# The last output product of every stage split by columns around the first turning of the next input

## The reference

```python
x = x + rms_norm(concat(gated, attention, conv) @ w_out, post_mix_g)        # moba
x = x + rms_norm(cross_attention(rms_norm(x, pre_x_g), m), post_x_g)        # cross
x = x + rms_norm(square(relu(rms_norm(x, pre_ffn_g) @ w_ff1)) @ w_ff2, g)   # relu
for i in range(2):                                                          # second block
    h = h + 0.5 * rms_norm(swiglu(rms_norm(h, g[0])), g[1])                 # glu0, glu2
    u = rms_norm(h, g[2])
    m = diff_attention(u) if i == 0 else neighborhood_attention(u)          # diff, near
    h = h + rms_norm(m, g[3])
    h = h + 0.5 * rms_norm(swiglu(rms_norm(h, g[4])), g[5])                 # glu1, glu3
```

## Time and profile before

| | |
|---|---|
| median of three runs | 1430.43 us |
| time of the profiled execution | 1429.05 us |
| its span in the trace | 1427.3 us |
| TensorE (PE) matmul busy | 1386.7 us (97%) |
| VectorE (DVE) busy | 816.4 us (57%) |
| ScalarE (ACT) busy | 704.5 us (49%) |
| GpSimd (POOL) busy | 144.3 us (10%) |
| granted TensorE clock | 0.997 of full |
| DMA, mean | 179 GB/s |

### The profile page before, as it was taken

The page is one execution under the profiler, slowest core; times in us unless marked ns, Lnnn a source line. Parts: engine busy times, 40 slices in busy tenths (PEclk is TensorE's granted clock), DMA queues, the critical chain, the costliest instruction groups (busy, mean ns, idle before and its releaser), DMA issues.

```text
span 1427.3 us, 17574 instructions
## 1 busy us (share of the span) xinstructions
PE 1386.7 (97%) x7129; PEld 1162.9 (81%) x7129; DVE 816.4 (57%) x900; ACT 704.5 (49%) x911; POOL 144.3 (10%) x254
## 2 busy tenths in 40 slices
PE   6999999999999999999999999999999999999996
PEld 6998788888888888877778888888888777788885
DVE  4986745645565444565765445654555556654552
ACT  5637654544455434465754444444344666544341
POOL 1000101111101111000111110021160100000000
PEclk9999999999999999999999999999999999999998
DMA  9854434865557655553348556485655533465530
GB/s 310 269 171 148 133 133 137 254 191 195 190 163 227 196 198 184 176 192 123 128 135 252 186 193 200 163 228 190 206 180 177 192 118 134 146 223 178 198 125 30
DMA packets 123421, 255.87 MB, mean 179 GB/s; under 512 B 6280, under 2 KB 36812, under 8 KB 123340
## 3 DMA queue, kind: packets, MB, share of 16 engines
q1 hardware_dynamic: 119244, 251.58, 54.3%
q0 software_dynamic: 4096, 3.15, 0.8%
HBM read 253.66 MB, written 1.05 MB: 178 GB/s over the span
## 4 chain that ended last, share of the span: by engine, by line
PE 88%; DVE 4%; ACT 3%; issue 3%; DMA 1%; POOL 0%; SPq 0%; DVEq 0%; POOLq 0%; ACTq 0%
PE ps L1159 25%; PE ps L1161 25%; PE ps L1160 25%; PE ps L1426 2%; ACT w_hi L595 2%; DVE w_lo L836 2%; PE ps L1147 1%; PE ps L1149 1%; PE ps L1148 1%; PE ps L1225 1%; DVE x_rows L883 1%; PE ps L1188 1%; PE ps L1265 1%; DMA raw<-w_in 1%; ACT t L654 1%
## 5 line engine op out<-in xcount | busy, mean ns | idle before, releaser
L836 DVE TENSOR_TENSOR w_lo<-raw,w_hi 128x2048 fp32r<-128x2048 f32 x226 | 518.5, 2296 | 423.4 <-ACT w_hi L595 422.9
L595 ACT CAST w_hi<-raw 128x2048 fp32r<-128x2048 f32 x226 | 430.3, 1907 | 396.7 <-PE ps L1161 382.4
L1159 PE MATMUL ps<-w_hi,hT_hi 128*128 128x512 f32 (+1 forms) x1168 | 442.1, 378 | 6.7 <-DVE w_lo L836 6.7
L1161 PE MATMUL ps<-w_hi,hT_lo 128*128 128x512 f32 (+1 forms) x1168 | 436.6, 374 | 0.0
L1160 PE MATMUL ps<-w_lo,hT_hi 128*128 128x512 f32 (+1 forms) x1168 | 436.0, 373 | 0.0
L1159 PE MATMUL ps<-w_hi,yT_hi 128*128 128x512 f32 (+1 forms) x672 | 258.3, 384 | 0.0
L1159 PEld LDWEIGHTS ps<-w_hi,hT_hi 128*128 128x128 f32 x1168 | 220.0, 188 | 46.6 <-DVE w_lo L836 8.6
L1161 PE MATMUL ps<-w_hi,yT_lo 128*128 128x512 f32 (+1 forms) x672 | 255.1, 380 | 0.0
L1160 PE MATMUL ps<-w_lo,yT_hi 128*128 128x512 f32 (+1 forms) x672 | 254.8, 379 | 0.0
L1161 PEld LDWEIGHTS ps<-w_hi,hT_lo 128*128 128x128 f32 x1168 | 219.9, 188 | 39.6
L1160 PEld LDWEIGHTS ps<-w_lo,hT_hi 128*128 128x128 f32 x1168 | 220.2, 189 | 37.1
(11 more groups left out here) (157 smaller groups left out, 1029.5 us busy)
## 6 DMA issues: line engine op xcount, KB each, us to landing
raw<-ffn_wg SPq DMA_DIRECT2D x44, 1024.0 KB, 5.5
raw<-ffn_wu SPq DMA_DIRECT2D x44, 1024.0 KB, 5.4
raw<-ffn_wd SPq DMA_DIRECT2D x44, 1024.0 KB, 5.2
raw<-w_ff SPq DMA_DIRECT2D x32, 1024.0 KB, 5.8
...
```

Of the source, the lines that this page charges most:

```text
L595: act.copy(hi_part(c), raw[:, c % NRAW, :]).then_inc(hi_done, 1)
L836: dve.tensor_tensor(lo_part(c), raw[:, c % NRAW, :], hi_part(c), ALU.subtract).then_inc(lo_done, 1)
L1159: pe.matmul(o, hi, wh[:, i, cols], start=first and i == 0, stop=False)
L1161: ins = pe.matmul(o, lo, wh[:, i, cols], start=False, stop=last and i == len(tiles) - 1)
```

## The change

Three things are changed in the words, and the code learns the new ones.

1. The last product word of every stage but glu3 is split by columns, and `turn0` with it: `d5.1a sq0 turna0 d5.1b post2 turnb0`. `turna0` is the turning of b = 0, `turnb0` that of b = 1. `sq0` now stands ahead of the turning. In moba the last product was `o2.1`, with `turn0 sq0` ahead of it. In diff, near and cross `turn0` stood ahead of `o3.1`, in relu ahead of `s da7.1 db7.1`.
2. `post2` is `post` for t = 1, now at the stage's end, ahead of `turnb0`. At the next head a new word `add1` does both additions to x for t = 1, ahead of the first split, and `gain1` does its two multiplications alone.
3. `HEAD_QK` (diff and near) has the split behind `tq0.1` moved behind `rk0.1`, where two now stand. In diff's fill table the casts `h` of step 2 and of steps 5 to 8, and the subtractions `l` of steps 6 to 9, stand later (the last cast in step 10, the last subtraction in step 11).

```diff
-HEAD_GLU = ("ga0.0 post1 s gb0.0 gain1 s ua0.0 turn1 sq1 ub0.0 G0.0 H0.0 ga0.1 s gb0.1 G0.1 s ua0.1 s "
+HEAD_GLU = ("ga0.0 add1 s gb0.0 gain1 s ua0.0 turn1 sq1 ub0.0 G0.0 H0.0 ga0.1 s gb0.1 G0.1 s ua0.1 s "
...
-           "tq0.1 s kb0.1 rk0.1 s va0.0 tk0.1 va0.1 h ")
+           "tq0.1 kb0.1 rk0.1 s s va0.0 tk0.1 va0.1 h ")
...
-    "glu1": GLU + "post0 gain0 da4.1 s db4.1 turn0 sq0 d5.1",
+    "glu1": GLU + "post0 gain0 da4.1 s db4.1 d5.1a sq0 turna0 d5.1b post2 turnb0",
...
-                                   5: "||h l|vd0.1 rv1", 6: "||h l|o0.0", 7: "||h l|o0.1", 8: "||h l|o1.0", 9: "||l|o1.1a",
-                                   10: "|||o1.1b", 11: "|||o2.0a"}) +
+                                   5: "||l|vd0.1 rv1", 6: "||h|o0.0", 7: "||l|o0.1", 8: "h||l|o1.0", 9: "h|||o1.1a",
+                                   10: "h|l||o1.1b", 11: "|l||o2.0a"}) +
...
+TURN_HALVES = {"turn": (0, 1), "turna": (0,), "turnb": (1,)}
...
-            j = word.at - word.digit
-            return word.digit, j, j + 2 if j < N_NORMS - 1 else None
+            j = word.at - (word.digit == 1)
+            return min(word.digit, 1), j, j + 2 if j < N_NORMS - 1 else None
...
-            def turned_hi(n, t, dst):
-                for b in range(2):
+            def turned_hi(n, t, dst, halves=(0, 1)):
+                for b in halves:
...
-                    if n is None:
-                        for b in range(2):
-                            add_y(j, t, b)
+                if word.name == "add" or n is None:
+                    for b in range(2):
+                        add_y(j, t, b)
                 if word.name == "gain":
                     for b in range(2):
-                        add_y(j, t, b)
+                        if t == 0:
+                            add_y(j, t, b)
                         gain_row(n, x, t, b)
...
-            def turn(n, t):
+            def turn(n, t, halves=(0, 1)):
...
-                for b in range(2):
+                for b in halves:
                     pe.wait_ge(normed, 2 * (TT * n + t) + b + 1)
```

More of the change, by code:

```diff
@@ L73 @@
 GLU = HEAD_GLU + "".join(BLOCK_GLU.format(a=b - 1, b=b) for b in range(1, 5)) + LAST_GLU
-HEAD_RELU = ("ua0.0 post1 s ub0.0 gain1 s ua1.0 turn1 sq1 ub1.0 G0.0 H0.0 ua0.1 s ub0.1 G0.1 H0.1 s ua1.1 T0 s "
+HEAD_RELU = ("ua0.0 add1 s ub0.0 gain1 s ua1.0 turn1 sq1 ub1.0 G0.0 H0.0 ua0.1 s ub0.1 G0.1 H0.1 s ua1.1 T0 s "
              "ub1.1 G1.0 H1.0 G1.1 H1.1 s da0 s db0 s ")
@@ L78 @@
         "ua7 s T6 ub7 G7.0 H7.0 G7.1 H7.1 s da6.0 T7 db6.0 da7.0 db7.0 ")
-HEAD_QK = ("qa0.0 post1 s qb0.0 gain1 s sq1 rq0.0 ka0.0 turn1 kb0.0 tq0.0 rk0.0 qa0.1 s qb0.1 tk0.0 rq0.1 s ka0.1 "
-           "tq0.1 s kb0.1 rk0.1 s va0.0 tk0.1 va0.1 h ")
+HEAD_QK = ("qa0.0 add1 s qb0.0 gain1 s sq1 rq0.0 ka0.0 turn1 kb0.0 tq0.0 rk0.0 qa0.1 s qb0.1 tk0.0 rq0.1 s ka0.1 "
+           "tq0.1 kb0.1 rk0.1 s s va0.0 tk0.1 va0.1 h ")
 PLAN = {
@@ L86 @@
                                  5: "||h l l|o3.0"}) +
-             "o2.0 post0 gain0 o3.1 turn0 sq0 o2.1"),
-    "cross": ("qa0.0 post1 s qb0.0 gain1 s sq1 rq0.0 qc0.0 turn1 qd0.0 tq0.0 rq1.0 qa0.1 s qb0.1 tq1.0 rq0.1 s qc0.1 "
+             "o2.0 post0 gain0 o3.1 o2.1a sq0 turna0 o2.1b post2 turnb0"),
+    "cross": ("qa0.0 add1 s qb0.0 gain1 s sq1 rq0.0 qc0.0 turn1 qd0.0 tq0.0 rq1.0 qa0.1 s qb0.1 tq1.0 rq0.1 s qc0.1 "
               "tq0.1 h qd0.1 rq1.1 exp " +
               attention("cross", 4, {0: "tq1.1|||", 4: "||l h|o0.0", 5: "||l|o0.1", 6: "||h l|o1.0"}) +
-              "o2.0 o3.0 post0 gain0 o1.1 h l o2.1 turn0 sq0 o3.1"),
-    "relu": RELU + "post0 gain0 da6.1 s db6.1 turn0 sq0 s da7.1 db7.1",
-    "glu0": GLU + "post0 gain0 da4.1 s db4.1 turn0 sq0 d5.1",
+              "o2.0 o3.0 post0 gain0 o1.1 h l o2.1 o3.1a sq0 turna0 o3.1b post2 turnb0"),
+    "relu": RELU + "post0 gain0 da6.1 s db6.1 s da7.1 db7.1a sq0 turna0 db7.1b post2 turnb0",
+    "glu0": GLU + "post0 gain0 da4.1 s db4.1 d5.1a sq0 turna0 d5.1b post2 turnb0",
     "diff": (HEAD_QK +
-             attention("diff", 8, {0: "||l|vb0 rv0", 1: "||h l|qc0 qd0.0 rq1.0", 2: "||h|qd0.1 rq1.1 l kc0.0 tq1 kc0.1",
+             attention("diff", 8, {0: "||l|vb0 rv0", 1: "||h l|qc0 qd0.0 rq1.0", 2: "|||qd0.1 rq1.1 h l kc0.0 tq1 kc0.1",
                                    3: "|||kd0.0 rk1.0 kd0.1 h tk1.0 rk1.1 l vc0.0 tk1.1 vc0.1", 4: "||h|vd0.0",
-                                   5: "||h l|vd0.1 rv1", 6: "||h l|o0.0", 7: "||h l|o0.1", 8: "||h l|o1.0", 9: "||l|o1.1a",
-                                   10: "|||o1.1b", 11: "|||o2.0a"}) +
-             "h l o2.0b o3.0 post0 gain0 o2.1 turn0 sq0 o3.1"),
-    "glu1": GLU + "post0 gain0 da4.1 s db4.1 turn0 sq0 d5.1",
-    "glu2": GLU + "post0 gain0 da4.1 s db4.1 turn0 sq0 d5.1",
+                                   5: "||l|vd0.1 rv1", 6: "||h|o0.0", 7: "||l|o0.1", 8: "h||l|o1.0", 9: "h|||o1.1a",
+                                   10: "h|l||o1.1b", 11: "|l||o2.0a"}) +
+             "h l o2.0b o3.0 post0 gain0 o2.1 o3.1a sq0 turna0 o3.1b post2 turnb0"),
+    "glu1": GLU + "post0 gain0 da4.1 s db4.1 d5.1a sq0 turna0 d5.1b post2 turnb0",
+    "glu2": GLU + "post0 gain0 da4.1 s db4.1 d5.1a sq0 turna0 d5.1b post2 turnb0",
     "near": (HEAD_QK +
@@ L106 @@
                                  9: "||l|o2.0b"}) +
-             "o3.0 post0 gain0 o2.1 turn0 sq0 o3.1"),
+             "o3.0 post0 gain0 o2.1 o3.1a sq0 turna0 o3.1b post2 turnb0"),
     "glu3": GLU + "post0 da4.1 db4.1 d5.1 end1",
@@ L808, in _ @@
                         split()
-                    elif word.name in ("post", "sq", "turn", "end"):
+                    elif word.name in ("post", "sq", "end") or word.name in TURN_HALVES:
                         norm_word(word)
@@ L1120, in _ @@
                         split()
-                    elif word.name in ("post", "gain", "sq", "turn", "end"):
+                    elif word.name in ("post", "add", "gain", "end") or word.name in TURN_HALVES:
                         norm_word(word)
```

14 lines of the change are left out of this document (7 added, 7 removed).

## The result

| | before | after |
|---|---|---|
| median | 1430.43 us | 1415.11 us (1414.64 to 1416.05, four runs) |
| time of the profiled execution | 1429.05 us | 1414.64 us |
| its span | 1427.3 us | 1412.8 us |
| ratio to the kernel before | | 0.9894, 95% interval 0.9877 to 0.9912 |

A forecast was written before the change was run, and what follows sets the result against it. TensorE, busy for 1386.7 of 1427.3 us, was taken as the bound, so only shorter waits help. Terms -5.4 - 8.8 - 1.3 + 1.2 + 0.4 + 0.2 = -13.7 gave a median of 1416.7 us; 8-in-10 range 1414 to 1420.5.

The forecast's parts named there:

- Half turnings: Stage ends of moba, diff and near: all of the 1.79 us lost in waits for `t` goes at each, -5.4 us.
- Second switch of instruction: Turning split in two: TensorE's additional switch between transposes and product costs 0.1 to 0.3 us over eight heads, taken as +0.2.
- The low part for the next product: Next stage's first product: its `hT_lo` is ready with 0.16 us left, so the cost is counted as 0.
- `post2`: Stage's end: second square of y at 916.74, the cast then as before, GpSimd's root there at 918.47 and short.
- `add1`: Stage heads: with both additions ahead of the first split, eight waits for `w_lo` go, 1.10 us each, -8.8.
- The 0.4 for the third chunk: Stage heads: the third chunk's load must also come in ahead of a matmul, 0.05 us at each head, +0.4.
- Rival A: Heads: VectorE's chain runs without overlaps, a wait of 0.3 to 0.6 us a head stays, 1421.5; 0.23 together with Rival C.
- HEAD_QK and step 2: Rotations in HEAD_QK and diff's step 2 no longer stand behind a `w_lo` or cast; two waits for `gain` go, -1.3 us.
- diff's later steps: Diff's fill: moved casts hold squares `A5` to `A7`, `o3.0` starts at 719.2 instead of 717.9, early gain spent, +1.2 us.
- Rival B: Diff keeps what its first steps gain, as `A7` is not held: -2 instead of +1.2, 1413.5 us; chance 0.10.
- Rival C: Inside the stages half of the heads' gain is given back, 4.4 us, 1421; chance 0.23 together with Rival A.
- E: Whole kernel: the change alters nothing, since another wait already stands behind those that go, 1430 us; chance 0.04.

The follow-up runs named there:

- late split: The changed kernel with the split `s` moved behind `sq0` in the tails of glu0, glu1 and glu2: 1417.37 us, ratio to the kernel before 0.9917.

## Why the prediction held

**Half turnings (-5.4).** By starts 1.8 in each of moba, diff and near, and no `t` was late anywhere. The kernel with the split alone shows the term by itself: 5.05.

**Second switch of instruction (+0.2).** It came, though in two parts of opposite sign. The end of glu2, from its last turn to products with `hT` (1075.00 before, 1064.43 after) to near's first product, takes 30.14 us before and 30.04 after: four transposes cost 0.36 twice where eight cost 0.79. But the first half product of each head now stands right behind four transposes, and takes 2.84 (907.41 to the line below) where it took 2.72: the second matmul starts 0.31 behind the first, the next ones 0.23 to 0.24 apart.

```profile
910.25 0.39 PE L1162 MATMUL ps<-w_hi,hT_hi 128*128 128x512 f32 x1
```

Together it is 0.03 a stage, 0.2 over eight heads. The term was taken from no row, so its size is luck.

**The low part for the next product (0).** Slack predicted 0.16, measured 0.24. The late split shows what stands behind it.

**`post2`.** The second square was put 0.27 ahead of the next first product and came 0.16 ahead (907.25, 907.41). The prediction's own 0.36 for four transposes gives 0.16 (917.21 less 0.36, against 917.01); its 916.74 was a slip of 0.1. GpSimd's root behind it took 0.30 us (908.04) beside a scaling that reads PSUM (907.97 to 908.66), as predicted. Without this step being right, the sum would have been 11 us off, as the kernel with `post` at the head shows.

**`add1` (-8.8 + 0.4).** Additions, `w_lo` and multiplications ran with the predicted overlaps: 909.18, 910.50, 912.70, 913.91, each 0.1 later behind the first product than predicted. The 0.4 for the third chunk did not come (its `w_lo` was 0.18 ahead, not 0.10). Here two misses met: the chain was 0.1 late, but the slow half product behind `turnb0` put off the third chunk's by 0.12, so that the margin held is luck in part. The 0.4 would have come, as 0.2 at each head, without `post2`. Rival A (VectorE's chain stays late) is so refuted for this order, but by 0.2 us.

**HEAD_QK and step 2 (-1.3).** Both waits for `gain` went: 1.50 by starts, 0.46 in HEAD_QK and 1.04 in step 2.

**diff's later steps (+1.2).** Measured +1.14: the lead of 7.71 us falls to 6.57 at the second matmul of `o3.0` (718.19 before, 711.62 after). TensorE, ScalarE and VectorE there, after the change, where it is 7.71 us ahead of the kernel before until head 4's turning (5.23 at diff's first product, 0.98 from the head, 1.50 from the two waits for `gain`):

```profile
696.07 0.63 PE L1228 MATMUL ps<-tab,prob 128*128 128x128 f32 x4 [1.13 <-DVE yT_lo L1073]
...
701.51 0.63 PE L1228 MATMUL ps<-tab,prob 128*128 128x128 f32 x4 [0.93 <-DVE yT_lo L1073]
...
705.86 0.27 ACT L672 ACTIVATE att_bias<-ps 128x128 f32<-128x128 f32 x1
...
707.70 0.61 DVE L1058 SCALAR_TENSOR_TENSOR att_bias<-ps,sub_stat,sub_gain 128x128 f32<-128x128 f32 x2 [0.89 <-POOL sub_stat L564]
...
708.79 0.41 PE L1282 MATMUL ps<-tab,att_bias 128*128 128x128 f32 x2 [1.15 <-DVE yT_lo L1073]
...
711.32 0.47 PE L1162 MATMUL ps<-w_hi,yT_hi 128*128 128x512 f32 x1 [0.73 <-DVE yT_lo L1073]
```

With 7.71 added: `A7` 713.57 (predicted 713.4), `B7` 715.41 (715.7), the last `Z` 716.50 (716.8), `o3.0` 719.03 (719.2). The one step that was off is the 2.26 from `A7` to `B7`, which measured 1.84: in the kernel before this root had lain beside a `w_lo` and its first instruction took 0.61, now 0.20. I had taken a distance over that included the lock. The prediction also left out the wait of 0.5 at head 6's `Z` in the kernel before, which went. Rival B (diff keeps its early gain) did not come; the old table in its place gives 0.13 more.

**Sum.** The sum missed by 0.7 us: the +0.4 that stayed out, and diff, where waits of 1.3 were worth 1.5 and the later steps cost a little less than 1.2. Rival C (given back inside the stages) did not come: a stage with a changed head keeps 1.0 to 1.1. Nor did E.

What stays open: the last 0.6 to 0.7 us in diff's late steps, and what made the granted clock fall in one trace and not in the others. Every place tried for `o3`'s `w_lo` meets either a low part or a root; whether one is clear of both is not known.
